# Six gate chunks of a wide projection as quarters inside three attention stages, and scores two deep instead of three

## The chip, the cores and the metric

The kernel runs on one core of a Trainium2 chip, in one launch. The metric is the device time of that core in microseconds (us). Engines in this text: TensorE (PE in rows; PEld are its weight loads), VectorE (DVE), ScalarE (ACT), GpSimd (POOL), SyncE (SP, which here only issues transfers), and the DMA engines.

## What is computed

A stream x of 256 tokens by 1024 channels passes through two blocks. The first has two layers (feed-forward, a mixer, cross-attention to a memory, feed-forward). The second, which the change touches, is in short:

```
u = rmsnorm(x, norm_mix) * (1 + scale1) + shift1
aq, ak, av, bq, bkv, biq, bik, biw, cq, ck, cv, g = split_cols(u @ w_in)   # g: 3072 columns
y_a = diff_attention(aq, ak, av, lam, subln, bias_a) @ w_br_a              # 4 heads, difference of two softmaxes
y_b = dsa_attention(bq, rmsnorm(bkv), biq, bik, biw, w_uv, bias_b) @ w_br_b # 4 heads, 64 keys chosen by an index score
y_c = moba_attention(cq, ck, cv, bias_c) @ w_br_c                          # 4 heads
gates = sigmoid(g + gate_b).reshape(B, S, 3, D)
merged = gates[0] * y_a + gates[1] * y_b + gates[2] * y_c
x = x + gate1 * (merged @ w_o)
x = x + gate2 * (square(relu(u2 @ w_ff1)) @ w_ff2)                          # u2: normed and modulated x
return rmsnorm(x, norm_final)
```

The gates g are needed only at `merged`, after all three attentions. The index scores biq, bik, biw choose the 64 keys of each query in the second attention (dsa).

## The kernel before

Each engine runs its own program through the same list of stages (`program(e)`), one method for each stage and engine. A stage begins with `enter()`, which waits until ScalarE and VectorE have left the one before, and ends on those two with `leave()`. Inside a stage, work is ordered by the order in which each engine's program lists it, with semaphores between engines; every engine works strictly in that order.

**Large matmuls.** Weights come in chunks of 1024 rows by 512 columns (4 transfers of 512 KB). A chunk takes a pair of slots, 0 and 1 or 2 and 3; a slot holds 512 rows. To keep fp32 accuracy each weight slot is split: SP loads `raw`, ScalarE copies it to `whi` in fp32r (line 722), VectorE writes `wlo = raw - whi` (line 1218); the activations have such parts too (`aT_hi`, `aT_lo`). Each product is then three matmuls (`parts`, lines 1865 to 1867). A chunk of rows is 2 token tiles x 8 x 3 = 48 matmuls of 512 columns, a turned chunk 96 of 256. `split(slot)` on ScalarE waits for the transfer and for the last use of `whi`; on VectorE it waits for ScalarE's. SP's next load of a slot waits for VectorE's subtraction. While chunk c is multiplied, `chunks` lets ScalarE and VectorE split chunk c+1; then both evict chunk c from PSUM, and an `after(c)` hook runs.

**`wide_inputs`** has ten chunks: gate 0, the index columns (392 wide), gates 1 to 5, aq, ak, av. VectorE adds each gate chunk to `bgate` (line 1591, which holds the gates' bias), and ScalarE applies the sigmoid (line 1002). The index scores are two sets of matmuls (`index_scores`, line 2200, behind chunks 2 and 5), rectified by ScalarE (line 1011) in PSUM banks 2, 3, 6 and 7. In `after`, VectorE sums them over heads (`index_sums`, lines 1616 to 1624), and chooses 64 keys by eight rounds of `max` and `match_replace` (`index_top`, lines 1629 and 1630): for the second 128 rows (256 columns wide) behind chunks 3 to 5, for the first (128 wide) behind chunks 6 to 8.

**Attention stages.** `diff_bias` turns a bias table by matmuls (line 2227) and copies it. `diff` works through eight units (four heads by two token tiles). A unit u is: `score(u)` on TensorE (line 2253); `top(u)` on VectorE, bias add and row maximum (line 1654); `exps(u)` on ScalarE (line 1031); `weigh(u)` on VectorE (lines 1664 to 1667); transposes on TensorE, `turn_probs` (line 2241); `keep(u)` on ScalarE, their copy (line 1047); `values(u)` on TensorE (line 2263); `out(u)` on ScalarE (line 1051). Scores run two units ahead, in three pairs of PSUM banks. `sparse_inputs` has three chunks (bq; bkv with cv; cq with ck), norms diff's result with a power on POOL in between (lines 1684 to 1700), transposes it (line 2289), and turns the next bias. `latent` norms bkv. `dsa(0)` and `dsa(1)` take the two token tiles, four units each (lines 1734 to 1752 on VectorE, 2308 on TensorE), and end with values of all heads together (2319), a copy (1107), the expansion by w_uv (2324) and its copy (1111). `moba` is like diff with one score (lines 1766, 2337, 2345).

**`merge`** splits the result (lines 1145, 1783), has ScalarE and VectorE split slots 0 and 1, and multiplies the three branches; VectorE multiplies each by its gates (lines 1795, 1797) and adds (1803). Splits for the first branch's slots 2 and 3 are made at the end of `sparse_inputs`.

Of the kernel before, what the change touches and what calls it, by code (L numbers as in the profile page):

```python
# [14 lines left out]
P = 128  # L15
# [85 lines left out]
def build(nc, A, out):  # L101
    ds = bass.ds
    with ExitStack() as ctx:
# [57 lines left out]
        stored, relu_made, index_read = sem("stored"), sem("relu_made"), sem("index_read")  # L161

# [43 lines left out]
        iqT = area[:, 10496:11008].rearrange("p (k s) -> p k s", k=2)  # L206
        ikT = area[:, 11008:11264]
# [17 lines left out]
        work = [xnf[:, 1056:1184], xnf[:, 1184:1440]]  # L225
# [39 lines left out]
        def program(e):  # L265

            for l in L:
# [17 lines left out]
                e.ffn(A["ffn2_w_in"][l], A["ffn2_w_out"][l])  # L285
# [8 lines left out]
            e.dsa(0)  # L294
            e.dsa(1)
# [10 lines left out]
        def _(sp):  # L306
# [45 lines left out]
            class Sp:  # L352
# [10 lines left out]
                def ffn(self, w_in, w_out):  # L363
# [83 lines left out]
                ada = diff_bias = diff = latent = dsa = skip  # L447

                def moba(self):
                    stages.next(2)  # L450

                def wide_inputs(self):
# [3 lines left out]
                    chunk(w, COLS["g"], 512, 0)  # L456
                    pieces(w, [(0, COLS["biq"], 256)] + [(256 + 32 * j, COLS["bik"], 32) for j in range(4)]
                           + [(384, COLS["biw"], 8)], 392, 2)
                    for c in range(1, 6):
                        chunk(w, COLS["g"] + 512 * c, 512, 2 * ((c + 1) % 2))  # L460
                    for c, n in enumerate(("aq", "ak", "av"), 7):
                        chunk(w, COLS[n], 512, 2 * (c % 2))
# [58 lines left out]
        def _(pool):  # L521
# [40 lines left out]
            class Pool:  # L562
# [23 lines left out]
                def ffn(self, w_in, w_out):  # L586
# [80 lines left out]
                def dsa(self, t):  # L667
                    enter()
# [21 lines left out]
        def _(act):  # L690
# [52 lines left out]
            def next_slabs(first=0):  # L743

                for s in range(first, first + 2):
                    split(s)
# [9 lines left out]
            class Act:  # L756
# [40 lines left out]
                def ffn(self, w_in, w_out):  # L797
# [29 lines left out]
                    next_slabs()  # L827
# [159 lines left out]
                def wide_inputs(self):  # L987
                    enter()

                    def evac(c, b):  # L990
                        if c == 1:
                            return act.activation(iqT, ps[:, b, :].rearrange("p (k n) -> p k n", k=2), ACT.Copy)
                        if c == 7:
                            act.wait_ge(dist_out, 16)
                            return act.activation(aqT[:, 0:2, :], ps[:, b, :], ACT.Copy, scale=0.125)
                        if c == 8:
                            return act.activation(akT[:, 0:2, :], ps[:, b, :], ACT.Copy)
                        if c == 9:
                            return act.activation(av[:, 0, :], ps[:, b, :], ACT.Copy)
                        at = slice(512 * max(c - 1, 0), 512 * max(c - 1, 0) + 512)  # L1000
                        act.wait_ge(dve_evac, chunk_no.n + 1)
# [1463 lines left out]
```

## Time and profile before

| | |
|---|---|
| time, median of 3 runs | 1955.89 us (1954.1 to 1958.25) |
| profiled execution, span | 1951.6 us |
| median less that span | 4.3 us |
| TensorE, VectorE, ScalarE busy | 1747.7, 1018.7, 826.7 us |
| matmul records of TensorE | 8447 |

The span is that of one profiled execution; a run's time has some microseconds more around it. All times in the rows are in us from the span's start, unless they say ns. A row of a timeline is: start, duration, engine, line of the kernel, operation, what it writes and reads, shapes, how many were merged, and in brackets the engine's idle time before it with what ended that. Matmuls are pipelined: the distance between starts, not the duration, tells their pace. The granted clock is a share of full speed: 1.00 is 2.4 GHz, 0.50 is 1.2 GHz.

### The profile page before, as it was taken

What the parts mean: (1) busy time and instruction counts of PE and PEld (TensorE: products, weight loads), DVE (VectorE), ACT (ScalarE), POOL (GpSimd) and SP (SyncE); (2) the same over time, 40 slices, a digit from 0 to 9 for tenths busy, and PEclk for the clock granted to TensorE, in tenths of its full rate; (3) what the DMA queues carried; (4) which work ended last, traced back from release to release, by engine and by line L of the source; (5) the groups of instructions that cost most, each with busy time, mean ns of one, the idle gap of its engine ahead of it and who ended that gap; (6) DMA issues with size and microseconds to landing.
All of it is one profiled execution on the core that took longest, in us unless ns stands there. A gap on an engine that the chain in (4) does not pass through costs nothing.

```text
span 1951.6 us, 22498 instructions
## 1 busy us (share of the span) xinstructions
PE 1747.7 (90%) x8447; PEld 1421.4 (73%) x8447; DVE 1018.7 (52%) x1239; ACT 826.7 (42%) x979; POOL 75.6 (4%) x122
## 2 busy tenths in 40 slices
PE   6999968799989999899899888999889896779996
PEld 6788857688868888798655576888677783558885
DVE  4545555454454545455666454545457653555444
ACT  4555523365543434334433333655334443314342
POOL 0000000000000000000000001000010010000000
PEclk9999989999989999999656798999989986789999
DMA  8565633566554556525344536655545520345550
GB/s 286 168 191 185 214 119 97 194 194 189 180 180 152 168 187 193 172 82 167 106 141 123 201 103 206 216 181 192 173 175 175 170 91 11 133 158 193 192 174 22
DMA packets 197807, 314.82 MB, mean 161 GB/s; under 512 B 16185, under 2 KB 120661, under 8 KB 197232
## 3 DMA queue, kind: packets, MB, share of 16 engines
q1 hardware_dynamic: 191824, 288.90, 45.1%
q0 software_dynamic: 5920, 25.06, 3.6%
q8 instruction: 41, 0.67, 0.1%
q14 instruction: 22, 0.18, 0.0%
HBM read 309.71 MB, written 4.21 MB: 161 GB/s over the span
## 4 chain that ended last, share of the span: by engine, by line
PE 85%; DVE 7%; ACT 2%; issue 2%; POOL 1%; PEld 1%; DVEq 1%; DMA 0%; PEldq 0%; ACTq 0%; POOLq 0%
PE ps L1865 24%; PE ps L1867 23%; PE ps L1866 23%; PE ps L2143 2%; PE ps L1911 2%; PE ps L2128 1%; DVE wlo L1218 1%; PE ps L1952 1%; PE ps L2037 1%; PE ps L2119 1%; DVE gain L1266 1%; PE ps L2139 1%; DVE xn L1288 1%; PE ps L2191 1%; ACT xn L778 1%
## 5 line engine op out<-in xcount | busy, mean ns | idle before, releaser
L1218 DVE TENSOR_TENSOR wlo<-raw,whi 128x2048 fp32r<-128x2048 f32 x255 | 579.0, 2290 | 305.1 <-ACT whi L722 304.4
L722 ACT ACTIVATE whi<-raw 128x2048 fp32r<-128x2048 f32 x255 | 481.2, 1910 | 177.6 <-PE ps L1867 163.2
L1865 PE MATMUL ps<-wlo,aT_hi 128*128 128x512 f32 (+1 forms) x1280 | 499.9, 391 | 18.9 <-issue 8.3
L1867 PE MATMUL ps<-whi,aT_hi 128*128 128x512 f32 (+1 forms) x1280 | 493.3, 385 | 0.0
L1866 PE MATMUL ps<-whi,aT_lo 128*128 128x512 f32 (+1 forms) x1280 | 493.1, 385 | 0.0
L1865 PEld LDWEIGHTS ps<-wlo,aT_hi 128*128 128x128 f32 x1280 | 243.9, 191 | 68.5 <-issue 10.5
L1867 PEld LDWEIGHTS ps<-whi,aT_hi 128*128 128x128 f32 x1280 | 243.2, 190 | 48.1
L1866 PEld LDWEIGHTS ps<-whi,aT_lo 128*128 128x128 f32 x1280 | 244.0, 191 | 45.2
L1865 PE MATMUL ps<-wlo,hT_hi 128*128 128x512 f32 x480 | 187.2, 390 | 8.4 <-DVE hT_lo L1327 6.0
L1867 PE MATMUL ps<-whi,hT_hi 128*128 128x512 f32 x480 | 187.0, 389 | 0.0
L1866 PE MATMUL ps<-whi,hT_lo 128*128 128x512 f32 x480 | 186.8, 389 | 0.0
L1865 PE MATMUL ps<-aT_lo,whi 128*128 128x256 f32 x600 | 173.1, 289 | 13.8 <-DVE wlo L1218 7.3
L1866 PE MATMUL ps<-aT_hi,wlo 128*128 128x256 f32 x600 | 172.0, 287 | 0.0
L1867 PE MATMUL ps<-aT_hi,whi 128*128 128x256 f32 x600 | 171.8, 286 | 0.0
L1865 PEld LDWEIGHTS ps<-aT_lo,whi 128*128 128x128 f32 x600 | 117.6, 196 | 16.0 <-ACTq L706 8.2
L1866 PEld LDWEIGHTS ps<-aT_hi,wlo 128*128 128x128 f32 x600 | 117.7, 196 | 0.1
L1867 PEld LDWEIGHTS ps<-aT_hi,whi 128*128 128x128 f32 x600 | 117.4, 196 | 0.0
L1865 PEld LDWEIGHTS ps<-wlo,hT_hi 128*128 128x128 f32 x480 | 90.1, 188 | 28.0 <-issue 6.9
L1911 PE MATMUL ps<-cst,xn 128*128 128x128 f32 x192 | 44.7, 422 | 69.9 <-DVE xn L1288 51.4
L1867 PEld LDWEIGHTS ps<-whi,hT_hi 128*128 128x128 f32 x480 | 90.1, 188 | 18.9
L1866 PEld LDWEIGHTS ps<-whi,hT_lo 128*128 128x128 f32 x480 | 90.1, 188 | 18.6
L1911 PEld LDWEIGHTS ps<-cst,xn 128*128 128x128 f32 x192 | 38.1, 224 | 77.2 <-issue 72.9
(274 smaller groups left out, 1445.8 us busy)
## 6 DMA issues: line engine op xcount, KB each, us to landing
raw<-in_ffn_w_in SPq DMA_DIRECT2D x176, 512.0 KB, 4.8
raw<-in_ffn_w_out SPq DMA_DIRECT2D x88, 512.0 KB, 4.3
raw<-in_w_ff SPq DMA_DIRECT2D x64, 512.0 KB, 4.8
raw<-in_ada_w SPq DMA_DIRECT2D x48, 512.0 KB, 4.7
raw<-in_w_in SPq DMA_DIRECT2D x48, 512.0 KB, 4.6
raw<-in_xattn_w_kv SPq DMA_DIRECT2D x32, 512.0 KB, 6.7
raw<-in_xattn_w_q SPq DMA_DIRECT2D x16, 512.0 KB, 5.4
raw<-in_xattn_w_o SPq DMA_DIRECT2D x16, 512.0 KB, 6.3
```

The costliest lines, as they stand in the source:

```text
L722: act.activation(to, of, ACT.Copy).then_inc(hi_ready[slot], 1)
L778: act.activation(junk, src[:, t, :], ACT.Square, accum_out=ssq[:, t:t + 1])\
L1218: dve.tensor_tensor(lo, of, hi, ALU.subtract).then_inc(lo_ready[slot], 1)
L1266: ins = dve.scalar_tensor_tensor(out=acc, in0=w, scalar=condT[:, k:k + 1], in1=acc, op0=ALU.mult, op1=ALU.add)
L1288: last = dve.scalar_tensor_tensor(out=to[:, t, :], in0=src[:, t, :], scalar=rstd[:, t:t + 1], in1=gain[:, m % 2, :], op0=ALU.mult, op1=ALU ...
L1865: pe.matmul(o, lh, rl, start=start, stop=False, skip_group_check=True)
L1866: pe.matmul(o, ll, rh, start=False, stop=False, skip_group_check=True)
L1867: return pe.matmul(o, lh, rh, start=False, stop=stop, skip_group_check=True)
L1911: last = pe.transpose(ps[:, b, P * k:P * k + P], xn[:, t, P * f:P * f + P], ident)
L1952: last = pe.transpose(ps[:, 6, S * k + P * t:S * k + P * t + P], hs[:, t, HI + P * k:HI + P * k + P], ident)
L2037: last = pe.matmul(ps[:, 6 + h % 2, S * j:S * j + S], vm[:, m, 256 * h + P * j:256 * h + P * j + P], PTc(h)[:, m, :], start=m == 0, stop=m ...
L2143: last = pe.matmul(o, v[:, m, 64 * g:64 * g + 64], nsaP[gi % 2][:, half::2, c:c + P], start=False, stop=j == 1 and m == t)
```

## The change

The six gate chunks leave `wide_inputs`, which keeps four chunks: index columns, aq, ak, av. Gates 0 and 1 move into `diff`, 2 and 3 into `dsa`, 4 and 5 into `moba`; there, each of a stage's eight units gets a quarter of a chunk, `gate_part` (one token tile, one slot: 12 matmuls of 512 columns), between the next unit's score and this unit's transposes. The quarters accumulate in PSUM banks 6 and 7 (in moba 3 and 7). So diff's scores lose their third pair of banks: they run one unit ahead instead of two. `dsa(0)` and `dsa(1)` become one stage of eight units. The splits for a stage's second chunk stand in units 0 and 1, those for the following stage's first chunk in units 6 and 7 (dsa: 5 and 6), behind the unit's own work on ScalarE and on VectorE. VectorE adds half a chunk to `bgate` at units 2, 4, 6 and the end. The sigmoids run in `merge`, three of 128x2048. The top-k of the second 128 rows runs whole behind chunk 2 of `wide_inputs`, the sums of the first 128 rows behind its last chunk, and their top-k in `sparse_inputs`, behind the norm of diff's result. The second `ffn` of layer 1 now prepares the index columns, which have six transfers for a slot.

```diff
-                e.ffn(A["ffn2_w_in"][l], A["ffn2_w_out"][l])
+                e.ffn(A["ffn2_w_in"][l], A["ffn2_w_out"][l], after=2 if l == 0 else 6)
...
-            e.dsa(0)
-            e.dsa(1)
+            e.dsa()
...
# SP
+                def gate(self, c):
+                    chunk(A["w_in_2"][0], COLS["g"] + 512 * c, 512, gate_place(c)[0])
+
+                def diff(self):
+                    stages.next()
+                    self.gate(0)
+                    self.gate(1)
...
# ScalarE, wide_inputs
-                        at = slice(512 * max(c - 1, 0), 512 * max(c - 1, 0) + 512)
-                        act.wait_ge(dve_evac, chunk_no.n + 1)
-                        return act.activation(bgate[:, :, at], bgate[:, :, at], ACT.Sigmoid)
...
-                    chunks(10, evac, transfers=[(1, 6)], after=rectify)
+                    chunks(4, evac, after=rectify)
...
# ScalarE, diff
                     exps(0)
-                    exps(1)
                     for u in range(8):
+                        if u + 1 < 8:
+                            exps(u + 1)
                         keep(u)
-                        if u + 2 < 8:
-                            exps(u + 2)
                         if u:
                             out(u - 1)
+                        if u < 2:
+                            split(2 + u)
+                        if u == 4:
+                            self.gate_used(0)
+                        if u > 5:
+                            split(u - 6)
                     out(7)
...
# ScalarE, dsa
+                    exps(0)
+                    for u in range(8):
+                        if u + 1 < 8:
+                            exps(u + 1)
                         keep(u)
+                        if u == 4:
+                            latent_out(0)
+                        if u == 5:
+                            out(0)
+                        if u < 2:
+                            split(u)
...
+                        if u in (5, 6):
+                            split(u - 3)
+                    latent_out(1)
+                    out(1)
...
# ScalarE, merge
-                    split(0)
-                    split(1)
+                    for br in range(3):
+                        g = bgate[:, :, 1024 * br:1024 * br + 1024]
+                        act.activation(g, g, ACT.Sigmoid).then_inc(gates_made, 1)
+                        if br < 2:
+                            split(br)
...
# VectorE, wide_inputs
+                        if c == 1:
+                            self.index_sums(1)
+                        if c == 2:
+                            self.index_top(1, TOPK // 8)
+                            self.choose_keys(1)
+                        if c == 3:
+                            self.index_sums(0)
...
# VectorE, diff
                     top(0)
-                    top(1)
                     for u in range(8):
+                        if u + 1 < 8:
+                            top(u + 1)
                         weigh(u)
-                        if u + 2 < 8:
-                            top(u + 2)
+                        if u < 2:
+                            split(2 + u)
+                        if u in (2, 4):
+                            self.keep_gate(0, u // 2 - 1)
+                        if u == 6:
+                            self.keep_gate(1, 0)
+                        if u > 5:
+                            split(u - 6)
+                    self.keep_gate(1, 1)
...
# VectorE, sparse_inputs, behind the norm of diff's result
+                            self.index_top(0, TOPK // 8)
+                            self.choose_keys(0)
...
# VectorE, moba, behind weigh_one(u) and top(u + 2)
+                        if u < 2:
+                            split(u)
...
+                        if u > 5:
+                            split(u - 4)
...
# TensorE
+                def gate_part(self, c, q):
+
+                    (pair, banks), t, s = gate_place(c), q // 2, q % 2
+                    if c and s == 0:
+                        pe.wait_ge(gate_kept, 2 * c + t - 1)
+                    if t == 0:
+                        pe.wait_ge(lo_ready[pair + s], uses.next(pair + s))
+                    tok = slice(t * P, (t + 1) * P)
+                    for r in range(4):
+                        k = 4 * s + r
+                        last = parts(ps[:, banks[t], :], aT_hi[:, k, tok], aT_lo[:, k, tok],
+                                     whi[:, pair + s, 512 * r:512 * r + 512], wlo[:, pair + s, 512 * r:512 * r + 512],
+                                     k == 0, k == KD - 1)
...
# TensorE, diff
                     score(0)
-                    score(1)
                     for u in range(8):
-                        if u + 2 < 8:
-                            score(u + 2)
-                        self.turn_probs(u, u % 2, 6, depth=3, banks=1)
+                        if u + 1 < 8:
+                            score(u + 1)
+                        self.gate_part(u // 4, u % 4)
+                        self.turn_probs(u, u % 2, 4, depth=3, banks=1)
                         if u:
                             values(u - 1)
...
# TensorE, dsa
+                        if u < 7:
+                            self.gate_part(2 + u // 4, u % 4)
+                        self.turn_probs(u, u // 4, 2 + u % 2)
+                        if u == 4:
+                            values(0)
+                        if u == 5:
+                            expand(0)
+                    self.gate_part(3, 3)
+                    values(1)
+                    expand(1)
```

## Rows read from the trace of the kernel before

**Rows 1.** The page, part 1: busy time and share of each engine.
```profile
PE 1747.7 (90%) x8447; PEld 1421.4 (73%) x8447; DVE 1018.7 (52%) x1239; ACT 826.7 (42%) x979; POOL 75.6 (4%) x122
```

**Rows 2.** Windows: wide projection, diff, dsa, moba (stretch, length, engines' busy, clock, DMA).
```profile
1430.00:1549.00 119.00, 117.98 (x680) 102.74 (x680) 74.28 (x99) 48.76 (x39) 2.35 (x4) 0.98 0.57 198
1552.60:1575.00 22.40, 17.12 (x68) 11.21 (x68) 12.94 (x64) 12.86 (x49) 0.76 (x1) 0.60 0.08 25
1616.90:1644.60 27.70, 17.91 (x50) 8.72 (x50) 9.05 (x40) 8.94 (x28) 0.00 (x0) 0.54 0.00 1
1647.60:1665.00 17.40, 16.16 (x52) 8.90 (x52) 6.17 (x32) 6.23 (x24) 0.00 (x0) 0.55 0.00 0
```

**Rows 3.** Timeline of VectorE in the wide projection: evictions, top-k, sums.
```profile
1457.36 0.42 DVE L1577 COPY area<-ps 128x256 f32<-128x256 f32 x1 [4.25 <-PE ps L1867]
...
1468.27 1.22 DVE L1591 TENSOR_TENSOR area<-area,ps 128x1024 f32<-128x1024 f32 x1 [3.98 <-PE ps L1867]
...
1492.89 0.42 DVE L1629 MAX8 xn<-xn 128x8 f32<-128x256 f32 x1
...
1496.82 4.49 DVE L1218 TENSOR_TENSOR wlo<-raw,whi 128x2048 fp32r<-128x2048 f32 x2
...
1516.35 2.67 DVE L1618 SCALAR_TENSOR_TENSOR xn<-ps,area,xn 128x128 f32<-128x128 f32 x7
...
1526.34 0.69 DVE L1582 TENSOR_SCALAR area<-ps 128x512 f32<-128x512 f32 x1 [2.47 <-PE ps L1867]
...
1529.81 4.49 DVE L1218 TENSOR_TENSOR wlo<-raw,whi 128x2048 fp32r<-128x2048 f32 x2
1537.86 0.69 DVE L1585 COPY area<-ps 128x512 f32<-128x512 f32 x1 [3.56 <-PE ps L1867]
```

**Rows 4.** Timeline of all engines, bias stage and diff.
```profile
1549.61 1.95 PE L2227 MATMUL ps<-gain,cst 128*128 128x512 f32 x4 [0.88 <-ACTq L706]
...
1557.30 0.47 PE L2241 MATMUL ps<-cst,xn 128*128 128x128 f32 x1 [3.46 <-DVE xn L1667]
...
1557.81 0.28 ACT L1047 ACTIVATE area<-ps 128x128 f32<-128x128 f32 x1 [0.68 <-PE ps L2241]
...
1558.98 0.42 DVE L1654 CUSTOM_DVE_ANT_0 xn<-ps,area 128x256 f32<-128x256 f32 x1
...
1560.79 0.47 PE L2241 MATMUL ps<-cst,xn 128*128 128x128 f32 x1
...
1562.52 0.28 ACT L1051 ACTIVATE hs<-ps 128x128 f32<-128x128 f32 x1 [0.18 <-PE ps L2263]
```

**Rows 5.** Timelines of ScalarE, VectorE and TensorE in the inputs between diff and dsa.
```profile
1575.27 3.72 ACT L722 ACTIVATE whi<-raw 128x2048 fp32r<-128x2048 f32 x2 [0.24 <-ACTq L706]
...
1577.56 4.48 DVE L1218 TENSOR_TENSOR wlo<-raw,whi 128x2048 fp32r<-128x2048 f32 x2
...
1591.00 4.49 DVE L1218 TENSOR_TENSOR wlo<-raw,whi 128x2048 fp32r<-128x2048 f32 x2
...
1596.12 1.03 PE L2289 MATMUL ps<-cst,hs 128*128 128x128 f32 x8
```

**Rows 6.** Timeline of dsa: from bias add to transposes, and the values.
```profile
1618.08 0.28 DVE L1734 TENSOR_TENSOR xn<-area 128x128 f32<-128x128 f32 x1
...
1619.34 0.48 PE L2241 MATMUL ps<-cst,xn 128*128 128x128 f32 x1 [1.20 <-DVE xn L1752]
...
1639.21 3.57 PE L2319 MATMUL ps<-hs,area 128*128 128x512 f32 x4 [0.47 <-ACT hs L1098]
```

**Rows 7.** Timeline of moba: an exponential and a weighting.
```profile
1649.06 0.49 ACT L1031 ACTIVATE xn<-xn,small 128x256 f32<-128x256 f32 x1
...
1649.39 0.29 DVE L1752 TENSOR_SCALAR xn<-xn,small 128x128 f32<-128x128 f32 x1
```

**Rows 8.** Timeline of TensorE at the start of the merge.
```profile
1668.79 0.76 PE L1865 MATMUL ps<-wlo,aT_hi 128*128 128x512 f32 x1 [3.42 <-issue]
...
1673.18 0.39 PE L1866 MATMUL ps<-whi,aT_lo 128*128 128x512 f32 x1
```

More of the change, by code:

```diff
@@ L445, in skip, with dsa @@
                     stages.next()
-                ada = diff_bias = diff = latent = dsa = skip
+                ada = diff_bias = latent = skip
+                def gate(self, c):
[4 more added lines that the diff above has]
+                    self.gate(1)
+                def dsa(self):
+                    stages.next()
+                    self.gate(2)
+                    self.gate(3)
                 def moba(self):
                     stages.next(2)
+                    self.gate(4)
+                    self.gate(5)
                 def wide_inputs(self):
@@ L826, in ffn @@
                         done.n[s] += (rounds, rounds, rounds - 1, 1)[s]
-                    next_slabs()
+                    next_slabs(transfers=after)
                     c_ffn.next(rounds)
@@ L1112, in dsa @@
+                    latent_out(1)
+                    out(1)
+                    self.gate_used(3)
+                    units.next(8)
+                    groups.next(2)
                     leave()
@@ new lines, in wide_inputs, with choose_keys, keep_gate @@
+                    chunks(4, evac, after=choose)
+                    leave()
+                def choose_keys(self, t):
+                    step(dve.tensor_scalar(sel[t], work[t].rearrange("p (k n) -> p k n", n=P), -2.0e38, NEG,
+                                           ALU.is_gt, ALU.mult))
+                def keep_gate(self, c, t):
+                    pair, banks = gate_place(c)
+                    if c == 0:
+                        dve.wait_ge(gate_b_in, 32)
+                    dve.wait_ge(gate_summed, 2 * c + t + 1)
+                    at = bgate[:, t, 512 * c:512 * c + 512]
+                    dve.tensor_tensor(at, at, ps[:, banks[t], :], ALU.add).then_inc(gate_kept, 1)
+                    if t:
+                        for s in range(2):
+                            done.next(pair + s)
@@ L2211, in wide_inputs @@
                         else:
-                            chunk(2 * (c % 2), 512, turned(b) if c in (7, 8) else rows(b))
-                        if c == 2:
+                            chunk(2 * (c % 2), 512, turned(b) if c < 3 else rows(b))
+                        if c == 1:
                             pe.wait_ge(act_evac, chunk_no.n - 1)
@@ L2311, in dsa @@
                     score(0)
-                    for u in range(4):
-                        if u + 1 < 4:
+                    for u in range(8):
+                        if u + 1 < 8:
                             score(u + 1)
-                        self.turn_probs(u, t, 2 + u % 2)
-                    units.next(4)
-                    pe.wait_ge(probs_kept, units.n)
-                    for m in range(t + 1):
-                        last = pe.matmul(ps[:, 4, :], kvn[:, m, :], PTd[:, :, m, :], start=m == 0, stop=m == t)
```

198 lines of the change are left out of this document (114 added, 84 removed).

## The prediction

> **What bounds the kernel now.** I read the page first: TensorE is busy 90% of the span, VectorE 52%, ScalarE 42% [rows 1]. Then the windows by stage, which the change touches: the wide projection takes 119 us with TensorE busy for 118 of them at clock 0.98, while the three attention stages take 22.4, 27.7 and 17.4 us at clocks 0.60, 0.54 and 0.55, with TensorE idle for 5.3, 9.8 and 1.2 us of them [rows 2]. So the projection is TensorE's, and the attention stages are a chain between engines, run largely at the lower of TensorE's two levels (1.2 GHz; full is 2.4). The idea has room: six gate chunks have 6 x 10.9 = 65.5 us of TensorE, one chunk of 48 matmuls being the distance of two evictions, 1457.36 to 1468.27 [rows 3]. What matters is what a unit of attention costs once it also carries a quarter of a chunk (10.9 / 4 = 2.73 us), and who else works in it.
>
> **Wide projection: what goes and what it uncovered.** Four chunks stay: the index one (120 matmuls of 256 columns), two turned ones (96 such, 11.5 us by the evictions at 1526.34 and 1537.86), one of rows (10.9). The first is then 14.4 us, and about 2 more because this stage begins at the low clock: 16.4. The two sets of index scores are some 1.4 and 1 us. But the top-k, which lay beside ten chunks, now lies beside few. After the third chunk's end (16.4 + 11.5 + 1.4 + 11.5 = 40.8 us) VectorE has, in this order: an eviction 0.7, eight rounds of top-k of 256 columns (four take 3.93, so 7.9), the selection 0.3, two splits 4.5, the last eviction 0.7, and the sums of the second index score 3.3 (2.67 for seven steps, 0.3 for each of the two around them) [rows 3]. That is 17.4, so the stage ends at 58.2, where TensorE alone would be done at 40.8 + 1 + 10.9 = 52.7. Before, it took 119 [rows 2] and 0.6 to the bias stage's first matmul at 1549.61 [rows 4]: 119.6. **Term: -61.4.**
>
> **What a split costs inside a unit.** A quarter needs its weights split: ScalarE copies the rounded part (1.9 us each, two in 3.72), then VectorE subtracts (2.25 each, two in 4.48) [rows 5]. Each stage takes on four (two slots for its second chunk at units 0 and 1, two for the next stage's first chunk at units 6 and 7; in the second stage at 5 and 6). Both engines work in order, and this decides. ScalarE's copy stands behind `keep(u)`, which waits for the transposes of unit u. VectorE's subtraction stands in front of the next `top` and `weigh`, and the transposes of unit u+1 wait for that `weigh`. So the split is in the chain from one unit's transposes to the next:
> - diff: transposes to the start of `keep` 0.5, keep 0.3 [rows 4]; the output copy of unit u-1 behind it ends near 1.1 at full clock (2.0 at the low one, 1560.79 to 1562.80 [rows 4]); copy 1.9, subtract 2.3; then `top` and `weigh`, together 1.8 (1558.98 to 1560.79 [rows 4]). Sum 7.1; without the output copy (unit 0) 6.8; where no `top` follows (6 to 7) 6.3.
> - second stage (dsa): 0.8 + 1.9 + 2.3, then bias add, maximum and weighting 1.25 [rows 6]: 6.2. For the second half of the rows 6.8, with the expansion copied in between (5 to 6) 7.2, and 5.8 without a `top`.
> - moba: 0.8, the exponentials 0.6 (0.49 and their sum's readout), 1.9, 2.3, weighting 0.5 (a reciprocal, then 0.29) [rows 7]: 6.1; 5.5 for 6 to 7.
>
> **What a unit costs without a split.** There TensorE sets it. Its own work is 17.1 us in diff, 16.2 in moba, and 10.4 in dsa (17.9 less values and expansion), nearly all at the low clock [rows 2]; halved and by eight this is 1.1, 1.0 and 0.65, so with 2.73: 3.9, 3.8 and 3.3 us. Scores two deep cost nothing here: a quarter stands between a score and its transposes, longer than `top` and `weigh` (1.8).
>
> **The stages.** Time of each unit's transposes from the stage's start:
> - diff: first 3.5 (scores, then a quarter; the exponential's table load falls away), then 10.3, 17.4, four at 3.9 to 33.0, 39.3. After the last come keep, copy, subtract and one gate eviction of 0.7: 6.1. Ends at 45.4 against 22.4. **+23.0.**
> - dsa, its two calls now one: 3.3, 9.5, 15.7, 18.9, 22.2, 26.6 (with the first half's values, about 1), 33.8, 39.6. Then the last quarter, values (3.57 at the low clock, 1.8 at full [rows 6]), two copies, expansion: 6.9. Ends at 46.5 against 27.7. **+18.8.**
> - moba: 3.5, 9.6, 15.7, 30.9, 36.4, then 5.7. Ends at 42.1 against 18.4 (17.4 and the last copy). **+23.7.**
>
> So 65.5 us of gates lengthen attention by the same 65.5: what the quarters fill, the splits give back.
>
> **Inputs between diff and dsa.** The second top-k (eight rounds of 128 columns; four take 2.8, so 5.7 [rows 3]) and its selection, 0.2, move in front of the two splits for the third chunk. These run 1591.00 to 1595.5 now, and TensorE is at its eight transposes until 1597.2 [rows 5]. Of 6.0 us, 1.7 is slack. **+4.3.**
>
> **At nothing.** The sigmoids move to the merge, in front of its splits. Three of 128x2048 (about 1.9 by the copy of that shape) and a table load delay the second slot's subtraction to some 10 us after TensorE's start at 1668.8; the first branch's 48 matmuls cover that. Without this cover the bound is the whole of it, 7 us. The weights' transfers: each slot's next one still starts when its subtraction ends, at least a unit before its copy; the attention stages now hardly transfer (1 GB/s in dsa), so SP is not late. `after=6` only counts the pieces that now come first. The other waits on PSUM (gate_kept) are released two units earlier. Six drains: under 0.3 each, some in slack.
>
> **The clock.** This price no row shows whole. At 1668.79 TensorE starts after 3.42 us of idleness, a matmul every 0.43 us, and reaches 0.23 by 1673.18 [rows 8]: nine or ten at 0.2 extra, 1.9 us for a cold start. Bounds: nothing, if no new one is exposed, and the low level throughout, which makes units 7.8, 7.2 and 7.7, or +68. New idleness ahead of exposed work: 5.5 us ahead of the first bias stage; at dsa's start a quarter now meets a clock that was low already; in a diff split unit 7.1 - 3.9 = 3.2, near the 3.42 above, ahead of unit 2. Three starts, **+6**. The row at 1673.18 is nearest, as the quarters are the same dense matmuls. The Trainium skill ("TensorE: Matmul & The Clock Gate", section "Why this matters for your kernels") warns that idle gaps between bursts bring the half rate back, so it speaks against splits that hold the bursts apart. The row agrees on the price of one return; by the page the gap of each split unit would count, some six more, for 11 us more.
>
> **Sum:** -61.4 + 23.0 + 4.3 + 18.8 + 23.7 + 6 = +14.4. The profiled execution's span is 1951.6, so 1966; the runs' median of 1955.9 lies 4.3 above that span, so **1970.3**. Ten split units at +-0.5 and clock terms of 0 to 11 give this case its own range, 1959 to 1981.
>
> **Rivals.**
> - **The splits hide, faster.** If the subtraction did not stand in the transposes' chain (hi parts long ready, VectorE at it during a quarter), every unit would be TensorE's: diff 3.5 + 7 x 3.9 + 3.4 = 34.2, dsa 34.1, moba 33.7, so +11.8, +6.4 and +15.3. With -61.4, +4.3 and 4 for clocks: -19.6, **1936**. For it: VectorE is busy for only 12.9, 9.1 and 6.2 us of these stages [rows 2], and 9.2 + 2.6 us more fit. Against: queue order, not occupancy, counts. It decides from split units of 5.0 us down (14.4 over ten). The Trainium skill ("Perfetto Trace Analysis", section "Optimization Strategy") says that interleaving regimes with different contended engines may pay; followed fully, it is this case. Chance 0.16.
> - **Half of that**, where some splits hide and others don't: about **1953**, no change. 0.10.
> - **The clock stays low** in attention: fp32 transposes and scores between quarters keep 0.5, as moba shows with TensorE 93% busy [rows 2]. +68: **2032**. Against: dense matmuls raise it within 4 us [rows 8], and a quarter is dense. 0.06.
> - **The sigmoids are not covered** in the merge: +7, **1977**, inside the range. 0.05.
> - The forecast: 0.63.
>
> **Numbers.** 1970.3; a measurement of this kernel tells some 0.2%, 4 us, from no change. Range 1945 to 1988: it holds the forecast's own range, the sigmoids and the half case, and leaves out the two cases of 0.16 and 0.06. Faster 0.19 (0.16, and 0.03 of the half case), same 0.08 (0.07 of it, and 0.01 of the forecast's low edge), slower 0.73.
>
> **What would show it.** Wide projection 58 us, its last DVE work the sums of 128 columns. Idle TensorE ahead of L2241's transposes in units 1, 2 and 7, of 3 us, released by DVE's weighting, with the sequence copy, subtraction, weighting ahead of it; in units 3 to 6 none. dsa as one stage of 46 us. The cq chunk starting some 4 us after the transposes. Merge of unchanged length with sigmoids inside. Wrong would be: split units of 5 us or less; quarters at 0.43 us per matmul beyond their first; or a late DMA in front of a copy.

## Result and profile after

The changed kernel takes 1977.8 us (median of 4 runs, 1976.1 to 1979.1) against 1956.2 for the kernel before: ratio 1.0107, 95% interval 1.0092 to 1.0121, so 21.6 us slower. The forecast was +14.4, the range 1945 to 1988. It was measured again beside later experiments: 1978.0, ratio 1.0097 (1.0082 to 1.0113). Each ratio below is to the kernel before, run beside that experiment (1957.8 to 1959.0 us). One of the ten runs of experiment 5 took 3380 us and is left out there.

The page after, part 1, answers to [rows 1]: TensorE has the same work, in a longer span (1973.9 us).

```profile
PE 1744.1 (88%) x8447; PEld 1422.6 (72%) x8447; DVE 1018.0 (52%) x1245; ACT 825.1 (42%) x975; POOL 77.0 (4%) x122
```

Windows of the changed kernel by stage, columns as in [rows 2]: wide projection, first bias stage, diff, the inputs between diff and dsa (with the bias stage behind them), dsa, moba.

```profile
1432.30:1490.70 58.40, 52.45 (x392) 49.39 (x393) 35.29 (x56) 20.03 (x20) 2.36 (x4) 0.94 0.58 203
1490.70:1495.60 4.90, 3.75 (x4) 1.19 (x5) 0.83 (x2) 0.60 (x1) 0.00 (x0) 0.61 0.17 65
1495.60:1541.90 46.30, 33.81 (x165) 25.11 (x165) 24.37 (x73) 19.61 (x53) 0.76 (x1) 0.93 0.22 68
1541.90:1585.50 43.60, 37.77 (x252) 36.05 (x252) 26.30 (x40) 13.27 (x11) 7.03 (x4) 0.92 0.51 174
1590.20:1639.40 49.20, 36.44 (x146) 26.79 (x146) 20.23 (x48) 16.04 (x32) 0.00 (x0) 0.86 0.25 86
1642.40:1684.00 41.60, 36.23 (x148) 25.04 (x148) 14.65 (x38) 12.34 (x28) 0.00 (x0) 0.92 0.14 51
```

The projection has halved, and each attention stage has grown by more than 20 us. TensorE is idle for 12.5 us of diff, 12.8 of dsa. The ledger, from the first matmul of each stage to that of the next, in us:

| stretch | before | after | difference | forecast |
|---|---|---|---|---|
| wide projection | 119.7 | 58.5 | -61.2 | -61.4 |
| first bias stage | 3.1 | 4.9 | +1.8 | in the clock term |
| diff | 22.4 | 46.2 | +23.8 | +23.0 |
| inputs between diff and dsa | 34.4 | 41.3 | +6.9 | +4.3 |
| second bias stage and latent | 7.4 | 7.15 | -0.3 | 0 |
| dsa | 27.7 | 49.2 | +21.5 | +18.8 |
| third bias stage | 3.0 | 3.0 | 0 | 0 |
| moba, to the merge's first matmul | 21.2 | 48.3 | +27.2 | +23.7 |
| merge | 30.2 | 30.7 | +0.5 | 0 |
| ahead of the wide projection | 1429.9 | 1432.2 | +2.3 | 0 |
| clock, spread over the rows above | | | | +6 |

The sum with -0.1 behind the merge is +22.3 (before rounding), the difference of the two spans. The row ahead of the projection is not the change's: profiled executions of other kernels with the same code up to there begin the projection at 1432.6 to 1438.1, and one with the code of before begins it at 1437.1.

Timeline of the changed kernel, all engines, one split unit of diff, from the transposes of unit 1 to those of unit 2 (the same columns as [rows 4]).

```profile
1505.73 0.44 PE L2358 MATMUL ps<-cst,xn 128*128 128x128 f32 x2 [2.72 <-DVE xn L1735]
...
1506.20 0.38 ACT L1064 ACTIVATE area<-ps 128x256 f32<-128x256 f32 x1 [0.79 <-PE ps L2358]
...
1506.48 0.27 ACT L1068 ACTIVATE hs<-ps 128x128 f32<-128x128 f32 x1
1506.64 1.92 ACT L738 ACTIVATE whi<-raw 128x2048 fp32r<-128x2048 f32 x1
1508.58 2.29 DVE L1275 TENSOR_TENSOR wlo<-raw,whi 128x2048 fp32r<-128x2048 f32 x1 [2.91 <-ACT whi L738]
1510.79 0.41 DVE L1722 CUSTOM_DVE_ANT_0 xn<-ps,area 128x256 f32<-128x256 f32 x1
...
1512.19 0.35 DVE L1735 SCALAR_TENSOR_TENSOR xn<-xn,small 128x128 f32<-128x128 f32 x1
...
1512.60 0.33 PE L2358 MATMUL ps<-cst,xn 128*128 128x128 f32 x1 [2.61 <-DVE xn L1735]
```

This is the chain that the prediction wrote out: transposes, `keep`, output copy, high part, subtraction (VectorE idle for 2.91 us ahead of it, waiting for ScalarE), `top`, `weigh`, transposes. It takes 6.87 us against a forecast of 7.1, and TensorE waits for its last 2.61. The seven distances between diff's eight transposes are 6.37, 6.87, 4.41, 4.08, 3.97, 4.04 and 6.38: forecast 6.8, 7.1, 3.9 four times, 6.3.

Timelines of TensorE, VectorE and ScalarE ahead of the third chunk in the inputs between diff and dsa (compare [rows 5]).

```profile
1563.44 1.04 PE L2406 MATMUL ps<-cst,hs 128*128 128x128 f32 x8
...
1564.30 4.49 DVE L1275 TENSOR_TENSOR wlo<-raw,whi 128x2048 fp32r<-128x2048 f32 x2
...
1568.94 0.36 PE L1962 MATMUL ps<-aT_lo,whi 128*128 128x256 f32 x1 [4.47 <-DVE wlo L1275]
```

The top-k now stands ahead of the subtractions, and they begin behind the first transposes, at 1564.30; in [rows 5] they were done (1591.00 and 4.49 more) before the transposes began at 1596.12. Hence 4.47 us of idle TensorE.

TensorE in the changed kernel: the first bias stage, dsa's last unit with its last quarter, moba's third unit with the quarter behind it, and the merge's first matmul (which answers to [rows 8]).

```profile
1490.72 3.75 PE L2344 MATMUL ps<-gain,cst 128*128 128x512 f32 x4 [5.20 <-issue]
...
1630.38 0.69 PE L2358 MATMUL ps<-cst,xn 128*128 128x128 f32 x2 [5.06 <-DVE xn L1839]
1630.72 0.78 PE L1962 MATMUL ps<-wlo,aT_hi 128*128 128x512 f32 x1
...
1635.57 1.98 PE L2431 MATMUL ps<-hs,area 128*128 128x512 f32 x4
...
1657.64 0.33 PE L2358 MATMUL ps<-cst,xn 128*128 128x128 f32 x1 [1.77 <-DVE xn L1839]
...
1659.65 0.80 PE L1962 MATMUL ps<-wlo,aT_hi 128*128 128x512 f32 x1
...
1665.43 0.41 PE L2358 MATMUL ps<-cst,xn 128*128 128x128 f32 x2 [0.29 <-issue]
...
1690.72 0.77 PE L1962 MATMUL ps<-wlo,aT_hi 128*128 128x512 f32 x1 [6.72 <-issue]
```

Here the low level (1.2 GHz) costs time. The four bias matmuls take 3.75 us where [rows 4] have 1.95; the last quarter of dsa takes 4.85 from 1630.72 to 1635.57 where experiment 1 below takes 3.1; and a whole unit of moba, without a split in it, takes 7.8 at a matmul every 0.43 us, where the same unit takes 4.7 in experiment 1.

Windows of the changed kernel in which the granted clock was 0.50, beside those: diff's last transposes with their values, the start of the inputs behind diff, and the start of dsa.

```profile
1535.50:1541.80 6.30, 2.31 (x9) 1.78 (x9) 2.89 (x2) 2.71 (x5) 0.00 (x0) 0.50 0.45 162
1541.80:1545.70 3.90, 3.90 (x18) 3.90 (x19) 3.82 (x3) 3.62 (x2) 1.19 (x1) 0.50 0.83 269
1590.20:1593.50 3.30, 3.29 (x10) 2.82 (x11) 1.54 (x8) 0.95 (x4) 0.00 (x0) 0.50 0.00 0
```

dsa's first transposes come 4.8 us after its start. In experiment 9, where that start ran at the full pace, they come after 3.3, as forecast.

Timelines of ScalarE's and VectorE's part in the merge: the sigmoids' table load, the two subtractions, and the first branch's product.

```profile
1690.12 1.28 ACT L1202 ACT_TABLE_LOAD   x1
...
1695.16 2.29 DVE L1275 TENSOR_TENSOR wlo<-raw,whi 128x2048 fp32r<-128x2048 f32 x1 [3.51 <-ACT whi L738]
...
1698.77 2.29 DVE L1275 TENSOR_TENSOR wlo<-raw,whi 128x2048 fp32r<-128x2048 f32 x1 [1.31 <-ACT whi L738]
...
1704.48 1.22 DVE L1892 TENSOR_TENSOR xn<-ps,area 128x1024 f32<-128x1024 f32 x1 [3.43 <-PEq L2516]
```

The second slot is ready at 1701.1, and the first branch's matmuls last until 1704.5: covered.

### The profile page after: what moved, and what is told of

It is laid out like the page before. It is cut to its first block, busy times and chain, and to the rows that moved or that the text cites. A ratio compares the mean times of both kernels' runs of the same rounds, so it can differ in the third digit from the quotient of the medians.

```text
span 1973.9 us, 22494 instructions
## 1 busy us (share of the span) xinstructions
PE 1744.1 (88%) x8447; PEld 1422.6 (72%) x8447; DVE 1018.0 (52%) x1245; ACT 825.1 (42%) x975; POOL 77.0 (4%) x122
## 4 chain that ended last, share of the span: by engine, by line
PE 82%; DVE 8%; ACT 3%; issue 3%; POOL 1%; PEld 1%; DVEq 1%; DMA 0%; PEldq 0%; ACTq 0%; POOLq 0%
PE ps L1962 23%; PE ps L1964 23%; PE ps L1963 23%; PE ps L2240 2%; PE ps L2008 2%; DVE wlo L1275 2%; ACT whi L738 1%; PE ps L2225 1%; PE ps L2049 1%; PE ps L2134 1%; PE ps L2216 1%; DVE gain L1323 1%; DVE xn L1345 1%; PE ps L2236 1%; ACT xn L794 1%
## 5 line engine op out<-in xcount | busy, mean ns | idle before, releaser
L1962 PE MATMUL ps<-wlo,aT_hi 128*128 128x512 f32 (+2 forms) x1280 | 506.0, 395 | 20.3 <-issue 11.2
L1963 PE MATMUL ps<-whi,aT_lo 128*128 128x512 f32 (+2 forms) x1280 | 496.3, 388 | 0.0
L1964 PE MATMUL ps<-whi,aT_hi 128*128 128x512 f32 (+2 forms) x1280 | 495.9, 387 | 0.0
```

The lines of the kernel that those rows point to most:

```text
L1962: pe.matmul(o, lh, rl, start=start, stop=False, skip_group_check=True)
L1963: pe.matmul(o, ll, rh, start=False, stop=False, skip_group_check=True)
L1964: return pe.matmul(o, lh, rh, start=False, stop=stop, skip_group_check=True)
```

## Experiments

All edits are to the changed kernel unless it says the kernel before. "Changed" below is the changed kernel.

**1. The subtraction one unit later.** The reason given for the loss is an order on VectorE, so that order alone is moved (diff; the other two stages alike):

```diff
-                        if u < 2:
-                            split(2 + u)
+                        if u in (1, 2):
+                            split(1 + u)
...
-                        if u > 5:
-                            split(u - 6)
+                        if u == 7:
+                            split(0)
+                    split(1)
                     self.keep_gate(1, 1)
```

> The changed kernel with one thing moved: in the three attention stages VectorE subtracts each slot's high part one unit later than ScalarE has copied it (units 1, 2 and 7 and behind the last unit, or 1, 2, 6, 7 in the second stage, in place of 0, 1, 6, 7 and 0, 1, 5, 6). The same work, the same waits between engines. Theory (the split stands in the chain from one unit's transposes to the next, because VectorE waits for a copy that ScalarE starts behind keep(u)): split units shrink from 6.1 to 7.8 us to about 4.3, TensorE's idle time of 1.2 to 2.9 us ahead of the transposes of units 1, 2, 7 is gone, the time falls by 20 to 28 us from 1977.8, to 1950 to 1958. Rival A (TensorE's own work, a quarter, scores, transposes and values, sets the units, and the idle time comes back elsewhere): no more than 5 us less. Rival B (the copy of 1.9 us on ScalarE alone keeps the unit long, as keep(u+1) and the exponentials stand behind it): units of 5.5, some 10 to 12 us less.

Measured: 1946.7 us, ratio to before 0.9941 (0.9917 to 0.9965), 31 us under the changed kernel and 12 under the kernel before. Its timeline, units 1 and 2 of diff:

```profile
1503.00 2.29 DVE L1275 TENSOR_TENSOR wlo<-raw,whi 128x2048 fp32r<-128x2048 f32 x1
...
1504.09 0.38 PE L2360 MATMUL ps<-cst,xn 128*128 128x128 f32 x2
...
1504.95 1.92 ACT L738 ACTIVATE whi<-raw 128x2048 fp32r<-128x2048 f32 x1
...
1507.05 2.28 DVE L1275 TENSOR_TENSOR wlo<-raw,whi 128x2048 fp32r<-128x2048 f32 x1
...
1508.13 0.27 PE L2360 MATMUL ps<-cst,xn 128*128 128x128 f32 x1
```

VectorE no longer waits for ScalarE, it subtracts while TensorE is in a quarter, and the units are 3.5 and 4.0 us. The idle time ahead of the transposes is gone. So ScalarE's copy in the same place costs nothing (rival B falls); only VectorE's wait for it did. By stage, against the changed kernel's second profile: diff -8.9 (46.1 to 37.3), dsa -13.6, moba with the bias stage ahead of it -8.1, merge -1.0, inputs and latent +2.0, sum -29.6. More went than the 20 to 28 expected, as the low-clock stretches of dsa (1.7) and moba (3.1) went with the gaps.

**2. The next stage's splits earlier as well.** On top of experiment 1. ScalarE at units 4 and 5, VectorE at 5 and 6, in all three stages (here ScalarE in diff):

```diff
-                        if u > 5:
-                            split(u - 6)
+                        if u in (4, 5):
+                            split(u - 4)
```

> As the run before it, and the next stage's two slots are copied at units 4 and 5 and subtracted at units 5 and 6 in all three stages, in place of units 6 and 7 (or 5 and 6): nothing but the last quarter's eviction is left behind the last transposes. Theory: a further 4 to 8 us less than with the late subtraction alone, about 1946 (the tails behind the last transposes shrink from 6.3 in the first stage by 3 to 4, in the third by 2 to 3, none in the second). Rival (the tails were covered by the next stage's entry and its first transfers, or the weights land too late for the earlier copy): no difference.

Measured: 1942.1 us, ratio 0.9918 (0.9889 to 0.9946), 4.7 us less than experiment 1 in the same runs. The windows of diff, dsa and moba:

```profile
1500.50:1533.80 33.30, 32.18 (x164) 24.36 (x164) 24.30 (x72) 18.71 (x52) 0.76 (x1) 1.00 0.38 122
1581.40:1617.60 36.20, 32.54 (x146) 24.46 (x146) 20.15 (x48) 15.59 (x32) 0.00 (x0) 0.95 0.34 117
1620.60:1657.40 36.80, 32.85 (x148) 23.28 (x148) 18.86 (x42) 16.53 (x32) 0.00 (x0) 0.99 0.16 57
```

TensorE is at work in 97, 90 and 89% of them, at a clock of 0.95 to 1.00 where [rows 2] have 0.54 to 0.60. Stage to stage they take 33.6, 36.2 and 36.9 us (with the entry to the merge) where the rival "the splits hide" was worked out as 34.2, 34.1 and 33.7. In the merge's entry TensorE is idle for 3.41 us, as before the change, not 6.72.

**3. The second top-k in a gap of VectorE.** It moves ahead of the first chunk's eviction, where VectorE was idle for 6.59 us.

```diff
+                    def choose(c):
+                        if c == 0:
+                            self.index_top(0, TOPK // 8)
+                            self.choose_keys(0)
...
-                    chunks(3, evac, after=norm_results)
+                    chunks(3, evac, before=choose, after=norm_results)
```

> The changed kernel with one thing moved: in the projections between the first and second attention stage, the second top-k (eight rounds of 128 columns and the selection) runs ahead of the first chunk's eviction, where VectorE is idle for 6.6 us, in place of behind the normalization of the first branch. Theory (the top-k stands in front of the two splits of the third chunk, which TensorE waits for, 4.5 us idle and a low clock behind it): 5 to 7 us less than 1977.8, and the stretch from 41.3 us back to about 34.5. Rival (the transposes of the first branch, which wait for the normalization, were the bound, and the normalization moves back by what the top-k takes): no more than 1 us.

Measured: 1973.5 us, ratio 1.0082 (1.0053 to 1.0110), 4.4 us under the changed kernel's two medians, a little short of the 5 to 7 expected. The interval overlaps the changed kernel's, so the gain rests on the trace. TensorE:

```profile
1568.38 1.03 PE L2411 MATMUL ps<-cst,hs 128*128 128x128 f32 x8
1569.17 0.36 PE L1967 MATMUL ps<-aT_lo,whi 128*128 128x256 f32 x1
```

The third chunk follows the transposes at once. The stretch takes 35.1 us against 41.3: 4.7 of idle time, and 1.5 because the chunk no longer begins at the low clock (12.6 against 14.1). The transposes come as early after the stage's start as in the changed kernel (21.7 us): the normalization did not move back. The low level fell elsewhere too: dsa took 51.1 us in place of 49.2, its first quarter wholly at 0.43 us per matmul, and moba 45.3 in place of 48.3, though neither stage was changed.

**4. All moves together.** The splits of experiment 2; both top-ks in gaps of the inputs between diff and dsa, the first one no longer in the wide projection; the second index sums ahead of that projection's last eviction.

```diff
-                        if c == 2:
-                            self.index_top(1, TOPK // 8)
-                            self.choose_keys(1)
+                    def sums(c):
                         if c == 3:
                             self.index_sums(0)
...
+                        if c in (0, 2):
+                            self.index_top(1 - c // 2, TOPK // 8)
+                            self.choose_keys(1 - c // 2)
```

> The late and early splits together with three moves of VectorE's work into its idle time: the first top-k (256 columns) leaves the wide projection for the gap ahead of the first eviction between the first two attention stages, the second top-k (128 columns) goes to the gap ahead of the third chunk's eviction there, and the second index sums go ahead of the last eviction of the wide projection. Theory (everything that the quarters filled was given back by the order on VectorE, none of it by TensorE's own work): the wide projection takes 53 to 54 us in place of 58.5, the stretch between the stages 35 to 37 in place of 41.3, and the time is 1927 to 1940, under the kernel before (1956) by 1% or so. Rival (the gates' TensorE time cannot be had back in attention, as its matmuls there run at the low clock or beside their own waits): 1955 or more.

Measured: 1928.7 us, ratio 0.9848 (0.9830 to 0.9866): 1.5% under the kernel before, 49 us under the changed one. Windows of the wide projection and of the inputs behind diff:

```profile
1432.70:1486.90 54.20, 52.51 (x392) 49.44 (x393) 27.87 (x31) 20.11 (x20) 2.35 (x4) 0.96 0.64 224
1523.60:1558.90 35.30, 32.70 (x248) 32.26 (x248) 33.46 (x64) 13.12 (x10) 7.03 (x4) 1.00 0.54 188
```

The wide projection is 4.2 us shorter (58.5 to 54.2), so that much was VectorE's top-k and sums; the prediction had 5.5 (58.2, TensorE alone 52.7). In the second window VectorE is busy for 33.5 of 35.3 us: it holds no more there.

**5. Quarters of one matmul.** Each quarter has one matmul in place of 12, so the gates leave out most of their sum; waits, copies and subtractions stay.

```diff
-                    for r in range(4):
-                        k = 4 * s + r
-                        last = parts(...)
+                    last = pe.matmul(ps[:, banks[t], :], aT_hi[:, 4 * s, tok], whi[:, pair + s, 0:512],
+                                     start=s == 0, stop=s == 1)
```

> The changed kernel with each quarter cut from 12 matmuls to one, the same waits, copies and subtractions; the gates of this block are then not what the reference computes. 24 x 11 matmuls at 0.227 us, 60 us of TensorE, are gone. Theory (splits bound the split units, and a unit without a split has a chain of its own of about 3 to 4 us with scores two deep): split units keep 5.5 to 7 us, and the time falls by only 15 to 25 us from 1977.8. Rival (TensorE's work bounds the attention stages): 55 to 65 us less, 1915 to 1923.

Measured: 1961.8 us, ratio 1.0022 (1.0011 to 1.0033). 60 us of TensorE's work left, 16 us came of it. The window of diff, and its unit from transposes 1 to transposes 2:

```profile
1498.10:1544.50 46.40, 21.90 (x76) 13.18 (x76) 24.31 (x72) 19.76 (x53) 0.76 (x1) 0.53 0.22 68
```

```profile
1508.00 0.69 PE L2355 MATMUL ps<-cst,xn 128*128 128x128 f32 x2 [4.64 <-DVE xn L1735]
...
1511.26 2.29 DVE L1275 TENSOR_TENSOR wlo<-raw,whi 128x2048 fp32r<-128x2048 f32 x1 [3.32 <-ACT whi L738]
...
1515.27 0.47 PE L2355 MATMUL ps<-cst,xn 128*128 128x128 f32 x1 [4.27 <-DVE xn L1735]
```

diff takes 46.4 us, as with full quarters (46.2): its split units have 6.6, 7.3 and 7.0 and its plain ones 3.9 to 4.1, at a clock of 0.53. Nearly all of the 16 us come out of dsa (43.2) and moba (38.9).

**6. Scores two deep, alone, in the kernel before.**

```diff
-                    score(1)
                     for u in range(8):
-                        if u + 2 < 8:
-                            score(u + 2)
+                        if u + 1 < 8:
+                            score(u + 1)
```

> The kernel before with one part of the change alone: in the first attention stage one score ahead in place of two, two pairs of banks in place of three, and the orders on ScalarE and VectorE that go with it. No gate work in the stage. Theory of the prediction: a score's way through the maximum, the exponential and the weighting (about 4.2 us at the low clock) is then exposed in each unit, 2.3 us now, so the first stage takes 30 to 37 us in place of 22.4, and the kernel 8 to 15 us more than 1956; that the same order costs nothing in the changed kernel is then the quarter's doing. Rival (the depth of the scores never mattered): within 2 us of the kernel before, and the price of the changed kernel's first stage is the splits' alone in any case.

Measured: 1968.1 us, ratio 1.0050 (1.0033 to 1.0067), 10 us more. The window of diff, and two of its transposes:

```profile
1559.80:1592.10 32.30, 16.71 (x68) 11.07 (x68) 13.03 (x64) 13.93 (x49) 0.76 (x1) 0.57 0.05 17
```

```profile
1571.60 0.48 PE L2239 MATMUL ps<-cst,xn 128*128 128x128 f32 x1 [1.86 <-DVE xn L1666]
...
1575.46 0.69 PE L2239 MATMUL ps<-cst,xn 128*128 128x128 f32 x2 [1.80 <-DVE xn L1666]
```

The stage takes 32.3 us in place of 22.4, and TensorE waits 1.8 us in each unit from 1 to 6. Experiment 2 has full quarters in the same order and takes 33.6: there 21.8 us of gate matmuls lie in the time that the shallower order opens, for 1.3 us. Without quarters the depth costs 9.9. Beside them TensorE is idle for only 1.1 us of the stage in experiment 2, which bounds what it can cost there; no run has quarters with scores three deep.

**7. TensorE kept at work in three gaps.** Matmuls of zeros into free banks: 20 ahead of the first bias stage, 16 ahead of the third chunk behind diff, 25 ahead of the merge.

```diff
+            def warm(b, n):
+                for _ in range(n):
+                    last = pe.matmul(ps[:, b, :], zero[:, 0:P], zero[:, :], start=True, stop=True)
...
+                        warm(bank(), 20)
```

> The changed kernel itself once more, beside the runs that are compared with it: 1974 to 1981.

> The changed kernel with TensorE kept at work in three of its gaps by matmuls of zeros into banks that are free, results unused: 20 ahead of the first bias stage (5.2 us idle), 16 ahead of the third chunk between the attention stages (4.5 us idle) and 25 between the last attention unit and the merge (6.7 us idle). No other work moves. Theory (a gap of 3 us and more brings TensorE's low clock back, and each such start costs about 1.9 us): the four matmuls of the bias stage take 1.95 us in place of 3.75, the third chunk and the merge begin at the full pace, and the time falls by 4 to 6 us from the changed kernel's run beside it. Rival (the clock term was not real, or the extra matmuls are in the way of what they wait for): a difference within 1.5 us, or more time.

Measured: 1978.0 us (ratio 1.0097) for the changed kernel, 1972.3 us, ratio 1.0072 (1.0058 to 1.0086), with the gaps filled. TensorE, filled:

```profile
1485.68 4.74 PE L1969 MATMUL ps<-zero 128*128 128x512 f32 x20
1491.07 1.96 PE L2354 MATMUL ps<-gain,cst 128*128 128x512 f32 x4 [0.64 <-issue]
```

```profile
1566.54 0.35 PE L1962 MATMUL ps<-aT_lo,whi 128*128 128x256 f32 x1 [0.80 <-DVE wlo L1275]
```

The bias matmuls are back at 1.96 us, 1.8 less; the third chunk takes 12.6 in place of 14.1; the merge 28.2 in place of 30.7. Three starts at the low clock cost 1.8, 1.5 and 2.5 us; 5 to 6 us came back. A fourth place shows that the low level can come without a price. In this profile it came in diff, behind a gap of 2.73 us ahead of unit 1's transposes:

```profile
1505.20:1508.60 3.40, 3.40 (x11) 2.35 (x8) 1.51 (x1) 1.86 (x2) 0.00 (x0) 0.50 0.33 116
```

From its first matmul to its last the quarter there took 4.0 us, where it takes 2.65 in the changed kernel behind a gap of 2.72. The unit took 6.87 us in both: TensorE waited less for the split behind it (1.06 us in place of 2.61). So the expectation's 3 us is no bound: shorter gaps were followed by the low level too.

**8. The sigmoids away.** Each is cut to a copy of one column.

> The changed kernel with each of the three sigmoids in the merge cut to a copy of one column, so the gates enter the result without their sigmoid. 5.7 us of ScalarE and a table load are gone. Theory (the first branch's 48 matmuls cover them): within 1.5 us of the changed kernel's run. Rival (they delay the splits behind them): 4 to 7 us less.

Measured: 1980.3 us (1977.0 to 1982.0), ratio 1.0105 (1.0089 to 1.0120), against 1978.0 for the changed kernel beside it. From the merge's first matmul to the transposes behind it 30.7 us in both. They were covered.

**9. The gaps that all moves leave.** 16 matmuls of zeros ahead of the transposes in `latent`, 12 ahead of the merge.

> The kernel with all of VectorE's moves, and matmuls of zeros in the two gaps that are left in it ahead of dense work: 16 ahead of the key transposes (4.15 us idle) and 12 between the last attention unit and the merge (3.4 us idle). Theory of the clock: the second stage's first quarter and the merge begin at the full pace, 3 to 4 us less than with the moves alone: 1924 to 1926. Rival (a start at the low clock costs nothing that can be measured there): 1928 to 1930.

Measured: 1926.8 us, ratio 0.9837 (0.9824 to 0.9851), between what the theory and the rival expected. The ratios of this kernel and of experiment 4 don't part; the traces do. Filled:

```profile
1562.80 3.89 PE L1973 MATMUL ps<-zero 128*128 128x512 f32 x16 [0.96 <-ACTq L722]
...
1567.99 0.48 PE L1966 MATMUL ps<-wlo,aT_hi 128*128 128x512 f32 x1
```

dsa's first quarter now begins at the full pace, but its last one no longer does (4.7 us from 1595.20 to the values, 3.1 in experiment 4): from the bias stage ahead of dsa to the one behind it 43.8 us in both. The merge takes 28.2 in place of 31.1. So one of the two fills paid.

## Why the prediction was right, and where its sizes were off

**Right, shown by experiments.** "What the quarters fill, the splits give back": experiment 1 moves nothing but VectorE's subtractions, and 31 us return. Experiment 5 is the counter-test: without 60 us of quarters the split units keep their length. The rival "the splits hide" had the right condition (high parts long ready) and nearly the right time, 1936 against 1942 in experiment 2; the changed kernel simply doesn't meet the condition. The Trainium skill ("Perfetto Trace Analysis", section "Optimization Strategy") has it that interleaving regimes with different contended engines may pay. Experiment 4 agrees, with 1.5%; the changed kernel shows that it depends on the order in each engine's queue.

**The terms.** The wide projection (-61.4 against -61.2) and diff (+23.0 against +23.8) hold to a microsecond. What was missed of +7.9 by spans:
- 2.3 lies ahead of the changed code, and varies from one profiled execution to the next.
- The clock term was 6 for three starts. Measured are 1.8 in the first bias stage, 1.6 at dsa's start, 0.7 at the start of the inputs behind diff, 1.5 in the third chunk there, 1.7 in dsa's last quarter and 3.1 in a unit of moba: 10.4, in six places, near the upper end of the prediction's 0 to 11. The failed step is "three starts": the bias stage and dsa's start were named rightly; the one in diff did not come (its quarters ran at full pace behind 2.7 and 2.6 us of idleness), and the other four were not seen, moba's least of all. The merge starts cold before and after, so it adds no start.
- Inputs behind diff: +4.3 against 4.7 without the clock, which is the top-k's share (experiment 3). The 0.7 lies ahead of the transposes, which come 21.7 us after the stage's start where they came after 21.0: the first chunk ran at a granted clock of 0.50 from 1541.8 to 1545.7, and before the change only from 1575.1 to 1577.5.
- dsa +18.8 against 18.2 and moba +23.7 against 24.1 without the clock, merge +0.5. Inside the stages smaller misses cancel, and that is luck: dsa's four split units took 5.5 to 6.9 us, each 0.3 to 0.5 less than forecast, its other parts 0.9 more in all; in diff the first two split units took 0.7 less together, the plain ones 0.9 more.
- A unit without a split was put at 3.9, 3.8 and 3.3 us. The prediction's own terms add up to 3.8, 3.8 and 3.4; measured are 4.0 to 4.4 in diff, 3.5 to 4.3 in moba beside the slow one, and 3.3 to 4.3 in dsa.

**The clock and the page.** The Trainium skill ("TensorE: Matmul & The Clock Gate", section "Why this matters for your kernels") warns of idle gaps between bursts; taken fully it would have made +11 more. The rows agree for gaps of 4 to 7 us, which experiment 7 fills with profit. For the gaps of 2.4 to 2.9 us in split units they go both ways: behind the first two of diff the changed kernel's quarters ran at a matmul every 0.23 us, behind one of dsa (2.45 us) the quarter began at 0.43, and the third of diff (2.91 us) was followed by the low level, with no quarter left behind it. Where a quarter did start low in a split unit it cost nothing, since the split sets the unit anyway (6.87 us in diff at either level, experiment 7). So the further 11 us did not come. What did was not in the rule as I read it: in moba two gaps of 1.77 us, a unit apart, were followed by 12 matmuls at 0.43 in both profiled executions of the changed kernel, in a unit that no split covers. Experiments 7 and 8, with moba's code unchanged, show the same (48.3 us each). In experiment 3 the low level came one unit earlier, where a split covers it, and moba took 3.1 us less. So these 3.1 us depend on where the low level falls, which the order of the work alone does not fix.

**At nothing.** The sigmoids: shown (experiment 8). The scores two deep: shown, and the prediction's reason for it too (experiments 2 and 6). Its other reason, that TensorE sets a unit without a split, holds in moba, where the quarters' absence shortens such units from 3.5 to 4.3 us to 1.8 to 3.1. In diff such a unit takes 4 us with or without its quarter. With it TensorE is idle for at most 0.26 us ahead of the transposes, so it sets the unit; without it TensorE waits 1.1 us, at a clock of 0.53, so the chain does. That the transfers are not late is read from the rows only: the copies at units 4 and 5 of experiment 2 found their weights landed.

## What to carry to other kernels

When work is laid into an idle engine's time, ask of each helper instruction that it needs on the other engines what stands behind it in their queues: a 2.3 us subtraction that waits for a 1.9 us copy behind `keep` cost ten units 1 to 3 us each, and the same subtraction one unit later cost nothing. A producer and a consumer on two in-order engines should be a step of the pipeline apart. Where time was lost, moving only the suspected instruction is a better test than taking work away: it gave 31 us and the faster kernel (1928.7 us with the other moves, against 1957.8 for the kernel before, run beside it).

## What the runs showed of the hardware

- Matmuls of zeros, results unused, keep the clock at the full level for what follows: a merge of 28.2 us against 30.7 to 31.1.
- A start at the low level can move: with dsa's first quarter warmed, its last began at 0.43 us per matmul, with the same instructions in between.
- The low level came after a gap of 5.06 us, after one of 2.45, after two of 1.77 and after the 2.91 ahead of diff's last transposes, and not after those of 2.72 and 2.61 in diff.
- The same gap can be followed by either level. In diff, 2.72 or 2.73 us of idleness ahead of unit 1's transposes were followed by a quarter at the full pace in the changed kernel, and by a granted clock of 0.50 in experiment 7, with the same instructions around it. The length of the last gap alone does not tell the level; what does stays open.
